# One 256 KB load for the token rows of an expert's block, half rows on neighbouring partitions, instead of two strided loads of 64 half rows each

## What is computed

```python
scores = jax.nn.sigmoid(xt @ w_router)              # 16 experts in 4 groups
# best group of 4, top 2 experts in it, weights normalised -> gates (tokens x 16)
act = silu(einsum('nd,edf->nef', xt, w_gate)) * einsum('nd,edf->nef', xt, w_up)
y = einsum('nef,efd->nd', act * gates[..., None], w_down)   # D 1024, F 512, 16 experts
```

## Time and profile before

| what | value |
|---|---|
| median of three runs | 1429.04 us (1424.86 to 1430.89) |
| profiled execution, its own time | 1433.1 us |
| its span, first to last instruction | 1431.3 us |
| PE busy | 1314.8 us, 92% |
| DVE, ACT, POOL busy | 483.4, 312.0, 257.9 us |
| queue q1 (SP) | 329.69 MB, 61.0% of the DMA engines' time |
| queue q10 (ACT) | 19.21 MB, 4.3% |
| expert stage of layer 0 | about 468 to 712 us |
| expert stage of layer 1 | about 1159 to 1414 us |

### The profile page before, as it was taken

One profiled execution on the slowest core, in us unless ns is written; L12 is line 12 of the kernel. 1 busy time (PEld: TensorE's weight loads), 2 busy tenths in 40 slices (PEclk: granted clock), 3 DMA queues, 4 the chain that ended last, 5 costly groups with the idle time before them and its releaser, 6 DMA issues.

```text
span 1431.3 us, 17567 instructions
## 1 busy us (share of the span) xinstructions
PE 1314.8 (92%) x6869; PEld 750.7 (52%) x6870; DVE 483.4 (34%) x885; ACT 312.0 (22%) x483; POOL 257.9 (18%) x225
## 2 busy tenths in 40 slices
PE   6999999999999959889999999998999999899777
PEld 2555445675545535544546554555655554455343
DVE  2324327772136101011144352586413531110112
ACT  2126515631000100000020662464100110000000
POOL 2730017721000100000028000683200010000001
PEclk9999999999999979999999999999999999999999
DMA  9898426654437899999983221576443578999997
GB/s 348 259 328 280 178 65 233 236 192 148 176 117 294 335 379 385 387 391 393 391 319 125 91 90 59 178 243 233 163 177 118 210 293 350 353 391 386 396 415 290
DMA packets 117050, 371.87 MB, mean 260 GB/s; under 512 B 18016, under 2 KB 33024, under 8 KB 100336
## 3 DMA queue, kind: packets, MB, share of 16 engines
q1 hardware_dynamic: 86496, 329.69, 61.0%
q0 software_dynamic: 6480, 21.95, 4.3%
q10 hardware_dynamic: 24000, 19.21, 4.3%
HBM read 341.40 MB, written 29.43 MB: 259 GB/s over the span
## 4 chain that ended last, share of the span: by engine, by line
PE 74%; DMA 15%; DVE 6%; issue 2%; ACT 2%; SPq 1%; ACTq 0%; POOL 0%; DVEq 0%
PE pG L1721 24%; PE pG L1713 10%; PE pS L1810 10%; PE pG L1828 6%; PE pG L1966 6%; DMA ring<-in_w_exp_up_dram 3%; DMA modb<-in_w_exp_up_dram 3%; DMA ring<-in_w_exp_down_dram 3%; PE pX L1651 3%; PE pX L1810 2%; DMA hT_gen<-x_scr 2%; PE pG L1684 2%; DMA ring<-in_w_in_dram 2%; PE pS L1752 1%; DVE ring L1306 1%
## 5 line engine op out<-in xcount | busy, mean ns | idle before, releaser
L1721 PE MATMUL pG<-hT_gen,ring 128*128 128x384 f32 x1024 | 339.6, 489 | 1.6 <-ACT hT_gen L1057 1.6
L1721 PEld LDWEIGHTS pG<-hT_gen,ring 128*128 128x128 f32 x1024 | 191.8, 190 | 141.5 <-issue 13.7
L1810 PE MATMUL pS<-ring,hT_gen 128*64 128x256 f32 x1344 | 154.8, 386 | 16.6 <-DMA ring<-in_w_exp_up_dram 8.0
L1713 PE MATMUL pG<-ring,hT_gen 128*128 128x512 f32 (+1 forms) x384 | 150.4, 548 | 4.0 <-DMA ring<-in_w_in_dram 2.3
L1810 PEld LDWEIGHTS pS<-ring,hT_gen 128*64 128x64 f32 x1344 | 104.7, 139 | 69.1 <-issue 17.2
L1587 DVE TENSOR_TENSOR hT_gen<-pS,hT_gen 128x256 f32<-128x256 f32 x32 | 19.2, 601 | 325.6 <-PE pS L1810 325.6
L1713 PEld LDWEIGHTS pG<-ring,hT_gen 128*128 128x128 f32 x384 | 72.1, 191 | 73.4 <-issue 65.1
L822 POOL DMA_INDIRECT ring<-y_scr,idx x12 | 11.4, 946 | 487.5 <-ACTq L1134 484.4
L1828 PE MATMUL pG<-ring,hT_gen 128*64 128x512 f32 x352 | 83.9, 620 | 11.8 <-DVE hT_gen L1590 8.3
L710 POOL TENSOR_TENSOR stat<-stat,half 128x1 f32<-128x1 f32 (+3 forms) x30 | 27.8, 926 | 311.4 <-DVE stat L1259 209.9
L1966 PE MATMUL pG<-ring,hT_gen 128*128 128x512 f32 x192 | 83.1, 592 | 0.0
(11 more groups left out here) (303 smaller groups left out, 1613.0 us busy)
## 6 DMA issues: line engine op xcount, KB each, us to landing
ring<-in_w_mod_dram SPq DMA_DIRECT2D x24, 2048.0 KB, 8.3
ring<-in_w_exp_up_dram SPq DMA_DIRECT2D x22, 2048.0 KB, 26.2
ring<-in_w_in_dram SPq DMA_DIRECT2D x20, 2048.0 KB, 8.9
ring<-in_w_exp_down_dram SPq DMA_DIRECT2D x20, 2048.0 KB, 24.5
ring<-in_w_exp_gate_dram SPq DMA_DIRECT2D x20, 2048.0 KB, 22.9
modb<-in_w_exp_up_dram SPq DMA_DIRECT2D x10, 2048.0 KB, 30.5
hT_gen<-in_w_exp_down_dram SPq DMA_DIRECT2D x10, 2048.0 KB, 30.0
rows_nw<-in_w_exp_gate_dram SPq DMA_DIRECT2D x10, 2048.0 KB, 29.3
```

The costliest lines, as they stand in the source:

```text
L1713: ins = pe.matmul(ps[:, 0:width], hT[:, k, t * P:(t + 1) * P], w[:, k, 0:width], start=(k == 0), stop=(k == KC - 1))
L1721: ins = pe.matmul(ps[:, 0:TOK], w[:, k, c0:c0 + P], src[:, k, :], start=(k == 0), stop=(k == nk - 1))
L1810: ins = pe.matmul(dst[64 * hf:64 * hf + 64, 0:256], x[:, k, :], w[k][:, 256 * hf:256 * (hf + 1)], start=(k == 0), stop=(k == KC - 1))
```

## The change

Each block is loaded by one transfer. Its source is read as 128 half rows in DRAM order, so the 256 KB are one contiguous piece, and half row h of token r goes to partition 2r+h. Before, half row h of token r went to partition 64h+r, which took one transfer of 64 half rows, 4 KB apart in DRAM, for each h. PE's transposes are the same instructions; their output now has tokens and halves interleaved, so DVE's copy reads PSUM at a stride of two floats instead of one, and writes the same `xT`. The semaphores count 16 for a block where they counted 32. The stores to `y_scr` stay as they were, two of 64 half rows each.

```diff
             def token_rows(row, dst, s):
-                for hf in range(2):
-                    sp.dma_start(dst[BLK * hf:BLK * (hf + 1), :],
-                                 x_scr[row * BLK:(row + 1) * BLK, 512 * hf:512 * (hf + 1)]).then_inc(s, 16)
+                sp.dma_start(dst, x_scr[row * BLK:(row + 1) * BLK, :].rearrange("r (h c) -> (r h) c", h=2)).then_inc(s, 16)
...
                         act.wait_ge(e_xTp, p * 3 + (NLOAD * L + c))
-                        for hf in range(2):
-                            act.dma_start(xrow[(b + 1) % 3][BLK * hf:BLK * (hf + 1), :],
-                                          x_scr[bass.ds(p * (3 * BLK) + (c + 4) * BLK, BLK),
-                                                512 * hf:512 * (hf + 1)]).then_inc(x_got[(b + 1) % 3], 16)
+                        act.dma_start(xrow[(b + 1) % 3],
+                                      x_scr[bass.ds(p * (3 * BLK) + (c + 4) * BLK, BLK), :].rearrange("r (h c) -> (r h) c", h=2)
+                                      ).then_inc(x_got[(b + 1) % 3], 16)
...
-                            for hf in range(2):
-                                act.dma_start(xrow_o[BLK * hf:BLK * (hf + 1), :],
-                                              x_scr[bass.ds(row + BLK, BLK), 512 * hf:512 * (hf + 1)]).then_inc(xo_got, 16)
+                            act.dma_start(xrow_o, x_scr[bass.ds(row + BLK, BLK), :].rearrange("r (h c) -> (r h) c", h=2)
+                                          ).then_inc(xo_got, 16)
...
                 def xT_src(b):
-                    return bank[b].rearrange("p (c a s) -> p c a s", c=4, a=2)
+                    return bank[b].rearrange("p (c s a) -> p c a s", c=4, a=2)
```

More of the change, by code:

```diff
@@ L1132, in _ @@
                 act.wait_ge(v_dma, act.snap(further) * 32 + Y0)
-                act.wait_ge(xo_got, act.snap(further) * 32 + 1)
+                act.wait_ge(xo_got, act.snap(further) * 16 + 1)
                 act.sem_inc(y_all, 1)
@@ L2015, in expert_of @@
                     if turned:
-                        pe.wait_ge(x_got[(b + 1) % 3], p * 32 + 32 * (XS[(b + 1) % 3] * L + (c + 2) // 3))
+                        pe.wait_ge(x_got[(b + 1) % 3], p * 16 + 16 * (XS[(b + 1) % 3] * L + (c + 2) // 3))
                         turn(bank[4], xrow[(b + 1) % 3], 2)
@@ L2040, in further_blocks @@
                             done = pe.snap(further)
-                            pe.wait_ge(xo_first, 32 * (L + 1))
-                            pe.wait_ge(xo_got, done * 32 + 1)
+                            pe.wait_ge(xo_first, 16 * (L + 1))
+                            pe.wait_ge(xo_got, done * 16 + 1)
                             pe.wait_ge(v_dve, done * 4 + 1)
```

## The result

The changed kernel takes 1404.5 us (median of four runs, 1402.0 to 1407.3) against 1427.9 us in the runs beside it: 0.9835 of the time, 95% interval 0.9818 to 0.9852. That is 23.4 us or 1.65% faster, ten times what was forecast. Its profiled execution has a span of 1400.1 us.

The account below looks back on a forecast made before the run. The weight stream was taken to bound both expert stages, except a dry stretch set by PE. Terms -1.15 - 0.55 - 0.8 + 0.15 = -2.35 us from 1429.04 gave 1426.7 us, range 1420.5 to 1432.5 us.

Parts of the forecast that it names:

- The transfers in the stream: Both saturated stretches: token rows take 13.5 us of engine time and would go somewhat faster, -0.8 us (0 to -1.6).
- Rival B: Saturated stretches: 64-partition transfers hinder weights more than their share; stream gains 6.7 us, time 1420.6 us; chance 0.11.
- Its marker: Sign in the profile after, 1225 to 1400 us: q10's share falling below 8%.
- The port rule: Transfers to 64 partitions reach half the ports; token rows would need 5.4 us less engine time; admitted as a rival only.
- The stretches that set the pace: From 480 to 610 us and 1219.7 to 1403 us the weight stream bounds the kernel, DMA share 1.01.
- the dry one in layer 1: Between 1212 and 1219 us the weight stream has run dry, share 0.19, and PE sets the pace; expected to stay.
- SP's issues: Fewer token-row issues start the weights earlier: -1.15 us in layer 0, -0.55 us (0 to -0.6) in layer 1.
- The wait of 14 us: PE's 14.04 us wait for token rows at 526.79 in layer 0; claimed not worth 14 us, and to stay.
- DVE's copy: PSUM read at a stride of 8 bytes, four copies on PE's path: +0.15 us (0 to +2.1).
- ACT: Each step loses one issue of some 0.6 us on ACT, hidden behind PE's up product: 0.
- Rivals A and C: A: issue no cheaper or stream no earlier, 1429 to 1431 us, 0.18; C: engines meet in DRAM, 1434 us, 0.09.

Follow-up runs that it names:

- e5: Changed kernel with each block's token rows in two contiguous transfers, 8 tokens to partitions 0 to 15 and 56 to partitions 16 to 127: 1420.4 us, ratio 0.996.
- e4: Changed kernel with two token-row transfers of 64 half rows from the old source, each to every second partition: 1406.0 us, ratio 0.985.
- v1: Changed kernel with the token rows of expert 4 loaded by ACT instead of SP, in both layers: 1406.8 us, ratio 0.984.
- v2: Changed kernel with the token rows of expert 4 loaded by ACT in layer 0 alone: 1402.3 us, beside 1402.0 us for the changed kernel.
- e1: Changed kernel with each block's token rows in two contiguous transfers to 64 partitions each: 1428.4 us, ratio 1.000.
- e2: Changed kernel with each block's token rows in two transfers by columns, each to all 128 partitions in 1 KB pieces: 1414.1 us, ratio 0.990.

## Why the prediction was wrong

**The step that failed** is "The transfers in the stream". It asked what the token rows' own 13.5 us of engine time would be at q1's rate, and got -0.8 us (0 to -1.6). It took for granted that a transfer costs the stream only its own share. The rows did not say that: q1's 396 GB/s in the earlier trace rows looked like the speed of the memory, and a faster rate was in the same trace, in a stretch of the kernel before with weight loads alone, 428 GB/s:

```profile
1140.00:1150.00 10.00, 8.95 (x48) 5.75 (x49) 6.41 (x28) 0.21 (x1) 0.00 (x0) 1.00 1.01 428
```

Had I set 396 beside 428, the gap of 7.5% over q1's 91% of 313 us of saturated stretches, 21 us, would have been a term to explain and a bound of the range. What the term stands at by the runs: over the two stretches of the earlier trace rows and the two of the profile after, the weight packets' time above the undisturbed 611 and 309 ns (16 KB and 8 KB), divided over the 16 engines, fell from 23.2 to 2.7 us. That is -20.5 us where the prediction had -0.8, and most of the result.

**Rival B had the mechanism**, "hinder the weights more than their share says", but priced it by the token rows' own engine time, 6.7 us, and so got 0.11 and a lower end of 1420.5. The argument against it, that the stores are of the same form, was wrong: they read SBUF, and the packet records show no slowing while they run. Its marker was wrong as well: q10's share fell only to 9.6%, what I had foreseen for the forecast itself. The loss was in q1.

**The port rule** of the Trainium skill (SBUF — State Buffer, the DMA port part) pointed the right way, and I used it for the token rows' own time alone. The page gives the rate of a transfer by itself; what the runs show is the cost to another queue's. They agree that two transfers to 0..63 and 64..127 are bad. They do not bear out that only the range covered decides: e5 covers 112 partitions in one transfer and is slow. The Trainium skill's DMA: Bandwidth & Descriptors, The descriptor swizzle, has each engine write to one port of its own in a 128-partition transfer. It gives no shares for transfers to 64 or 112 partitions, and its shares of a weight load are not the consecutive ones that e5's expectation supposed; no trace here names a port or an engine's partitions. So the port is a candidate and not shown. What is shown is that the partitions written to decide, at the same bytes, source and number of transfers (e4 against the kernel before).

**What held.** The stretches that set the pace, layer by layer, were the right ones, and the dry one in layer 1 is still there (DMA share 0.55 from 1186 to 1200 us). SP's issues: forecast -1.15 (0 to -1.7) and -0.55; the first weights came 1.7 us and 0.8 us sooner behind the token rows. Whether all of it reaches the end is not settled: e4, which keeps two issues and has the fast stream, is 4.0 us above the changed kernel on the same chip, but the intervals just overlap, and its stages differ from that one's by only -0.5 and +1.5 us. The wait of 14 us was covered: v1 and v2 take it away and PE waits for weights in its place. With the stream faster it shrank to 10.3 us, and taking it away was worth 1 to 3 us in the stage. DVE's copy: forecast +0.15 us, measured 0. The Trainium skill's rule on lines of 8 bytes (Advanced Engine Details and Errata, PSUM Cachelines), whose slowdown it states for matmuls, does not carry over to this copy: 692 ns against 691. ACT: no one waited for its issues.

**Rivals A and C** fell with the issue times and with q10's share.

## What to carry to other kernels

When a stretch keeps the DMA engines at a share of 1, read the GB/s in it against the best that the same kind of transfer reaches anywhere in the trace; a gap is a term to explain, worth up to (gap) x (length of the stretch), however few bytes the disturber moves. Beside this stream of 128-partition loads, small loads to all 128 partitions or to every second one did no harm; small loads to a block of 64, or to blocks of 16 and 112, did. The first two forms are the ones to try. A wait of PE's in such a stretch is worth only what the stream allows; take it away last.

## What the runs showed of the hardware that was not expected

- 4% of the bytes, loaded to a block of 64 partitions at a time, made the weight packets 9% longer on average (16 KB packets 671 ns instead of 616) and up to 30% while they were in flight. Each 2 KB packet itself was only slightly slower (92 ns on average in q10 instead of 85).
- The time to issue one transfer went with its form in a way that bytes do not explain. On ACT (median): 64 half rows 527 ns (e1) and 542 ns (e4), 128 half rows of 2 KB 392 to 420 ns, 128 pieces of 1 KB 388 ns (e2), 16 and 112 half rows 386 ns (e5). On SP, 592 to 596 ns for 64 half rows against 330 for 128. The cause was not looked for.
- Cutting the pieces to 1 KB (e2) left the weights alone (618 ns a packet) but made the token rows land later: 20.1 us after their issue instead of 13.0 (medians), and 27.9 us for one further block, where the changed kernel's took 14.8 at most.
